# Zero products at five norms, a third weight unit of the second expert ahead, masks between the projection chunks

## What is computed

```python
def first_block(x, ...):
    for i in range(2):
        h = rmsnorm(x, norm_mix[i])
        y = gated_deltanet_bidir(h, ...) if i == 0 else dilated_window_attention(h, ...)
        x = x + y
        x = x + squared_relu_mlp(rmsnorm(x, norm_mlp[i]), w1[i], w2[i])   # 1024 -> 4096 -> 1024
    return rmsnorm(x, norm_final)

def gated_deltanet_bidir(h, w_in, conv_w, ...):
    qkv, z, ab = split(h @ w_in)                 # 3072, 1024, 32 columns
    qkv = silu(conv over 5 tokens (qkv))
    ...                                          # gated delta rule, both directions, chunked
def second_block(x, c, positions, ...):
    cos, sin = rope_tables(positions, 32)
    for l in range(2):
        sh1, sc1, g1, sh2, sc2, g2 = split(silu(c) @ w_mod[l] + b_mod[l])
        h = rmsnorm(x, norm1_g[l]) * (1 + sc1) + sh1
        x = x + g1 * ((three gated branches of h @ w_in[l]) @ w_out[l])
        h2 = rmsnorm(x, norm2_g[l]) * (1 + sc2) + sh2
        x = x + g2 * ec_moe(h2, ...)             # 16 experts, each takes its 32 best tokens
def ec_moe(h, w_router, w_gate, w_up, w_down):   # each weight 1024 x 1024 per expert
    ...
    y = (silu(xg @ w_gate[e]) * (xg @ w_up[e])) @ w_down[e]
```

## Time and profile before

| | us |
|---|---|
| median of 3 runs | 2377.35 |
| lowest and highest | 2376.77, 2383.16 |
| the profiled execution | 2378.3 |
| its span | 2376.3 |

### The profile page before, as it was taken

One profiled execution on the slowest core, in us unless ns is written; L12 is line 12 of the kernel. 1 busy time (PEld: TensorE's weight loads), 2 busy tenths in 40 slices (PEclk: granted clock), 3 DMA queues, 4 the chain that ended last, 5 costly groups with the idle time before them and its releaser, 6 DMA issues.

```text
span 2376.3 us, 34628 instructions
## 1 busy us (share of the span) xinstructions
PE 1977.1 (83%) x14616; PEld 1365.1 (57%) x14616; DVE 916.6 (39%) x1646; ACT 632.9 (27%) x1065; POOL 32.5 (1%) x51
## 2 busy tenths in 40 slices
PE   8898889999889998999886666667999886666665
PEld 7776758878557886898642222224888752222221
DVE  5655645668463766545410000002554520000001
ACT  3322344431134443374320000002374420000000
POOL 0100000000000000000000000000000000000000
PEclk9989999999999999999798888888999889888888
DMA  9301135769754775523599999999442669999997
GB/s 325 125 27 38 38 133 187 285 222 339 282 203 142 261 255 188 197 72 126 228 387 425 427 427 426 427 425 399 161 142 107 248 267 425 427 426 426 427 426 311
DMA packets 150883, 641.88 MB, mean 270 GB/s; under 512 B 9374, under 2 KB 30904, under 8 KB 117622
## 3 DMA queue, kind: packets, MB, share of 16 engines
q1 hardware_dynamic: 144474, 637.13, 67.9%
q10 hardware_dynamic: 6300, 3.20, 0.5%
HBM read 639.21 MB, written 1.10 MB: 269 GB/s over the span
## 4 chain that ended last, share of the span: by engine, by line
PE 57%; DMA 33%; DVE 5%; ACT 2%; issue 2%; DVEq 1%; SPq 1%; POOL 0%; ACTq 0%; POOLq 0%
DMA ring<-in_w_down 33%; PE psum L1377 6%; PE psum L992 5%; PE psum L993 5%; PE psum L994 5%; PE psum L1513 4%; PE psum L1095 3%; PE psum L691 3%; PE psum L1367 2%; PE psum L1256 2%; PE psum L1255 2%; PE psum L1257 2%; PE psum L1112 1%; PE psum L761 1%; PE psum L1246 1%
## 5 line engine op out<-in xcount | busy, mean ns | idle before, releaser
L1493 PE MATMUL psum<-ring,arena 128*32 128x256 f32 x4096 | 292.5, 438 | 169.3 <-DMA ring<-in_w_up 130.1
L1493 PEld LDWEIGHTS psum<-ring,arena 128*32 128x32 f32 x4096 | 142.1, 123 | 322.1 <-issue 144.7
L1513 PE MATMUL psum<-ring,arena 128*32 128x512 f32 x1024 | 161.8, 763 | 95.3 <-DMA ring<-in_w_down 86.0
L992 PE MATMUL psum<-arena_r 128*128 128x512 f32 x512 | 206.2, 403 | 11.8 <-DVE arena_r L1937 7.1
L2341 DVE TENSOR_TENSOR arena<-psum,arena 128x256 f32<-128x256 f32 x32 | 13.6, 425 | 524.5 <-PE psum L1493 524.5
L994 PE MATMUL psum<-ring_r,arena_r 128*128 128x512 f32 x512 | 203.5, 397 | 0.0
L1626 DVE TENSOR_TENSOR ring_r<-ring,arena_r 128x2048 fp32r<-128x2048 f32 x64 | 143.7, 2287 | 85.7 <-ACT arena_r L2413 85.6
L2348 DVE TENSOR_TENSOR arena<-psum,arena 128x512 f32<-128x512 f32 x64 | 44.3, 692 | 267.8 <-PE psum L1513 266.5
L1513 PEld LDWEIGHTS psum<-ring,arena 128*32 128x32 f32 x1024 | 32.3, 124 | 189.3 <-DMA ring<-in_w_down 101.9
L2847 ACT ACTIVATE arena<-psum 128x256 f32<-128x256 f32 x32 | 12.3, 385 | 476.1 <-PE psum L1493 476.1
L2413 ACT CAST arena_r<-ring 128x2048 fp32r<-128x2048 f32 x64 | 119.5, 1903 | 71.6 <-PE psum L994 71.6
(11 more groups left out here) (404 smaller groups left out, 3399.5 us busy)
## 6 DMA issues: line engine op xcount, KB each, us to landing
ring<-in_w_up SPq DMA_DIRECT2D x64, 2048.0 KB, 26.1
ring<-in_w_down SPq DMA_DIRECT2D x64, 2048.0 KB, 26.5
ring<-in_w_gate SPq DMA_DIRECT2D x60, 2048.0 KB, 26.6
ring<-in_mlp_w SPq DMA_DIRECT2D x32, 2048.0 KB, 8.5
ring<-in_w_mod SPq DMA_DIRECT2D x24, 2048.0 KB, 11.3
ring<-in_w_in SPq DMA_DIRECT2D x20, 2048.0 KB, 8.4
ring<-in_gdn_w_in SPq DMA_DIRECT2D x8, 2048.0 KB, 18.0
ring<-in_dswa_w_in SPq DMA_DIRECT2D x9, 1536.0 KB, 13.2
```

The costliest lines, as they stand in the source:

```text
L992: mm(o, xh, wh, start=start, stop=False, skip_group_check=True)
L1493: ins = mm(PS[32 * j:32 * j + 32, 4 + m, 0:T], XG[:, k, 0:CAP] if first else XGE[:, k, :], W(v + 2 * m + u, D)[:, kk, j * T:(j + 1) * T], ...
L1513: ins = mm(PS[32 * j:32 * j + 32, (7, 4)[half], :], HTE[:, k % 2, 32 * (k // 2):32 * (k // 2) + 32], W(v + 4 + u, D)[:, j, half * 512:(hal ...
```

## The change

Three things are done together.

**Zero products.** `keep_busy(n, b)` issues n products of 128x128 by 128x256 in f32, both operands the one column of zeros `zero1` repeated, into PSUM bank b, with no wait ahead. There are 2 before the transposes of MLP 0, 10 before those of MLP 1, 18 and 11 before those of the two layers of the second block, and 6 between the two halves of the attention norm. PE waits for POOL's first memsets once, at the start.

**Third unit.** A new buffer `NEXT2` takes the first half of w_up of expert 1. SP issues it before the first unit of expert 0, ACT copies it into its slot behind the two gate units, and SP's `expert(1, 3)` begins with the second up unit. To make room, the scratch space for GpSimd's own transfers, which the kernel has none of, is set to 256.

**Masks and loads.** `masks_and_angles` is cut in five and run behind the convolutions of chunks 10, 12, 14, 16 and 18. On SP the three `PMC` loads go behind the units `U_QKV + 1` and `U_QKV + 2`, which move ahead of them. PE waits for the ten small loads ahead of the decay sums.

```diff
@@ -191,6 +191,7 @@
 
         slots = [both(f"ring{i}", [P, SLOT]) for i in range(RING)]
         ring, ring_r = [s[0] for s in slots], [s[1] for s in slots]
+        NEXT2 = sb("next_up", [P, SLOT])[:]
         X = sb("x_resid", [P, TT, D])
         XN, XN_R = both("x_normed", [P, TT, D])
         HT, HT_R = both("h_featmajor", [P, KC, T])
@@ -451,10 +452,6 @@
             sp.dma_start(ALOG, A["gdn_a_log"].rearrange("a b c -> a (b c)").partition_broadcast(P)[:, 0]).then_inc(sem("params_in"), 16)
             load(U_AB, cols(A["gdn_w_in"][0], 4096, 4128))
             load(U_QKV, cols(A["gdn_w_in"][0], 0, 512))
-            for name, width in (("b_mod_2", 96), ("norm1_g_2", 16), ("norm2_g_2", 16)):
-                at = PM_AT[name]
-                sp.dma_start(PMC[:, at:at + width].rearrange("p (m k) -> p m k", k=KC),
-                             A[name].rearrange("l (m p k) -> p (l m) k", p=P, k=KC)).then_inc(sem("gdn_in"), 16)
             sp.dma_start(CUM, A["k_gdn"][:, 0:2 * P].rearrange("p (a b) -> p a b", b=P)).then_inc(sem("gdn_in"), 16)
             sp.dma_start(NEGM, A["k_gdn"][:, 2 * P:4 * P].rearrange("p (a b) -> p a b", b=P)).then_inc(sem("gdn_in"), 16)
             sp.dma_start(EYE32, A["k_gdn"][:, 4 * P:4 * P + Q32]).then_inc(sem("gdn_in"), 16)
@@ -462,7 +459,13 @@
             sp.dma_start(NW, A["gdn_norm_w"].partition_broadcast(P)[:, 0]).then_inc(sem("gdn_in"), 16)
             for t in range(TT):
                 sp.dma_start(POSI[:, t:t + 1], A["positions_2"][0, t * P:(t + 1) * P].rearrange("(p a) -> p a", a=1)).then_inc(sem("gdn_in"), 16)
-            for u in range(1, 8):
+            load(U_QKV + 1, cols(A["gdn_w_in"][0], 512, 1024))
+            load(U_QKV + 2, cols(A["gdn_w_in"][0], 1024, 1536))
+            for name, width in (("b_mod_2", 96), ("norm1_g_2", 16), ("norm2_g_2", 16)):
+                at = PM_AT[name]
+                sp.dma_start(PMC[:, at:at + width].rearrange("p (m k) -> p m k", k=KC),
+                             A[name].rearrange("l (m p k) -> p (l m) k", p=P, k=KC)).then_inc(sem("gdn_in"), 16)
+            for u in range(3, 8):
                 load(U_QKV + u, cols(A["gdn_w_in"][0], 512 * u, 512 * (u + 1)))
 
             def mod(g):
@@ -547,14 +550,15 @@
                     for u in range(2):
                         load(U_SEC + V_MOE + 4 + u, two(A["w_down_2"])[u * 512:(u + 1) * 512, :].rearrange("(j p r) n -> p j (r n)", p=P, r=2), tu + e)
 
+                second = pmajor(one(A["w_gate_2"])[1])
+                sp.dma_start(NEXT2.rearrange("p (k n) -> p k n", n=D), pmajor(one(A["w_up_2"])[1])[:, 0:4, :]).then_inc(sem("next0_in"), 16)
                 expert(0, 0)
-                second = pmajor(one(A["w_gate_2"])[1])
                 sp.dma_start(NEXT0.rearrange("p (k n) -> p k n", n=D), second[:, 0:4, :]).then_inc(sem("next0_in"), 16)
                 for part, ks in ((1, slice(6, 7)), (2, slice(7, 8))):
                     sp.dma_start(NEXT1[part].rearrange("p (k n) -> p k n", n=D), second[:, ks, :]).then_inc(sem("next1_in"), 16)
                 sp.wait_ge(sem("router_mm"), L + 1)
                 sp.dma_start(NEXT1[0].rearrange("p (k n) -> p k n", n=D), second[:, 4:6, :]).then_inc(sem("next1_in"), 16)
-                expert(1, 2)
+                expert(1, 3)
                 with sp.Fori(2, NE) as e:
                     expert(e, 0)
             sp.dma_start(LAST_ROW, A["final_g_2"].rearrange("(a d) -> a d", a=1).partition_broadcast(P)[:, 0]).then_inc(sem("fgr_in"), 16)
@@ -632,11 +636,18 @@
             def used(ins, n):
                 ins.then_inc(w_free[n % RING], 1)
 
-            def norm(k, pm=False):
-
+            def keep_busy(n, b):
+
+                for _ in range(n):
+                    mm(bank(b, T), zero1.to_broadcast([P, P]), zero1.to_broadcast([P, T]), start=True, stop=True, skip_group_check=True)
+
+            def norm(k, pm=False, before=0, between=0):
+
+                keep_busy(before, 4)
                 pe.wait_ge(sem("xn0"), k + 1)
                 for t in range(TT):
                     if t == 1:
+                        keep_busy(between, 0)
                         pe.wait_ge(sem("xn1"), k + 1)
                     for dc in HT_ORDER if t == 1 else range(KC):
                         o = pair(4 + dc // 2, P)[:, (dc % 2) * 2 + t]
@@ -672,6 +683,7 @@
 
 
             pe.wait_ge(sem("params_in"), PARAMS)
+            pe.wait_ge(sem("filled"), 1)
             for n, group in enumerate(ROWS):
                 cnt = sum(x for _, x in group)
                 ins = nc.tensor.transpose(PS[:, 3, n * P:n * P + cnt], ROWS_IN[0:cnt, n * P:(n + 1) * P], ident[0:cnt, 0:cnt])
@@ -721,6 +733,7 @@
 
             def decay_sums():
 
+                pe.wait_ge(sem("gdn_in"), 16 * 10)
                 pe.wait_ge(sem("gs_ready"), 1)
                 for d in range(2):
                     rhs = GS[:, :, d * 8:(d + 1) * 8]
@@ -1050,6 +1063,7 @@
                             ins = nc.tensor.transpose(pair(6 + cc // 2, P)[:, (cc % 2) * 2 + t], RL[u % 2][:, t, cc * P:(cc + 1) * P], ident)
                     ins.then_inc(sem("rl_turned"), 1)
 
+                keep_busy((2, 10)[l], 4)
                 norm_split(k_norm, 0)
                 up(0, 0, 0)
                 up(1, 0, 1)
@@ -1074,7 +1088,7 @@
                 return
 
 
-            norm(2)
+            norm(2, between=6)
 
             def relative():
 
@@ -1234,7 +1248,7 @@
             for L in range(NL):
                 tu = L * SEC_TURNS
                 u2 = U_SEC
-                norm(L * 2 + 4, True)
+                norm(L * 2 + 4, True, before=(18, 11)[L])
 
                 def tok(n, w, b):
 
@@ -1676,21 +1690,27 @@
                 dst = KN[:, ch - GH] if ch < 2 * GH else V[:, ch - 2 * GH]
                 v.tensor_copy(dst, pair(4 + ch % 2, P)[:, 0:2]).then_inc(sem("tok_done"), 1)
 
-            def masks_and_angles():
+            TWO_PI = 2.0 * math.pi
+            c1 = 6.28125
+            c2_ = 0.0019350051879882812
+            c3 = TWO_PI - c1 - c2_
+            BIG = 12582912.0
+
+            def masks():
 
                 dve.wait_ge(sem("gdn_in"), 16 * 10)
                 v.tensor_copy(marks[:], MSTAGE)
 
-                TWO_PI = 2.0 * math.pi
-                c1 = 6.28125
-                c2_ = 0.0019350051879882812
-                c3 = TWO_PI - c1 - c2_
-                BIG = 12582912.0
+            def angles():
+
                 v.tensor_copy(POSF, POSI[:])
                 settle()
                 for t in range(TT):
                     v.tensor_scalar(ANG[:, t, :], freq, POSF[:, t:t + 1], None, ALU.mult)
                 settle()
+
+            def turns():
+
                 v.tensor_scalar(KRD, ANG, 1.0 / TWO_PI, BIG, ALU.mult, ALU.add)
                 settle()
                 v.tensor_scalar(KRD, KRD, BIG, None, ALU.subtract)
@@ -1698,12 +1718,18 @@
                 for cst in (c1, c2_, c3):
                     v.scalar_tensor_tensor(ANG, KRD, -cst, ANG, ALU.mult, ALU.add)
                     settle()
+
+            def quarter_turn():
+
                 v.tensor_scalar(COS, ANG, math.pi / 2, None, ALU.add)
                 settle()
                 v.tensor_scalar(KRD, COS, math.pi, None, ALU.is_gt)
                 settle()
                 v.scalar_tensor_tensor(COS, KRD, -TWO_PI, COS, ALU.mult, ALU.add)
                 settle()
+
+            def limits():
+
                 lim = 3.1415925
                 v.tensor_scalar(COS, COS, lim, -lim, ALU.min, ALU.max)
                 v.tensor_scalar(ANG, ANG, lim, -lim, ALU.min, ALU.max).then_inc(sem("angle_in"), 1)
@@ -1746,7 +1772,6 @@
                 v.tensor_tensor(flat(KD_S), PS[:, 6, 32:64], flat(GC), ALU.subtract).then_inc(sem("decay_in"), 1)
 
             decay_logits()
-            masks_and_angles()
             for ch in range(24):
                 conv(ch)
                 if ch - 3 >= GH:
@@ -1755,6 +1780,16 @@
                     decay_steps()
                 elif ch == 7:
                     decay_totals()
+                elif ch == 10:
+                    masks()
+                elif ch == 12:
+                    angles()
+                elif ch == 14:
+                    turns()
+                elif ch == 16:
+                    quarter_turn()
+                elif ch == 18:
+                    limits()
                 elif ch == 21:
                     keys_scaled()
             for ch in (21, 22, 23):
@@ -2854,7 +2889,7 @@
                 gathered(0, 0, 2 * CAP, first_place)
                 expert(0, 0)
                 gate0, gate1 = u2 + V_MOE, u2 + V_MOE + 1
-                act.wait_ge(sem("next0_in"), L * 16 + 16)
+                act.wait_ge(sem("next0_in"), L * 32 + 32)
                 a.copy(ring[gate0 % RING][:, 0:SLOT], NEXT0).then_inc(w_full[gate0 % RING], 16)
                 act.wait_ge(sem("next1_in"), L * 48 + 48)
                 at = 0
@@ -2862,6 +2897,8 @@
                     ins = a.copy(ring[gate1 % RING][:, at:at + part.shape[1]], part)
```

(4 more changed lines are left out.)

## The result

The changed kernel takes 2361.02 us in the median of four executions (2357.07 to 2366.59) against 2377.06 of the kernel before: ratio 0.9936, 95% interval 0.9922 to 0.9951, that is 15.2 us (11.6 to 18.5) less. The forecast was 2361.9 us, 15.5 us less. In a second series on one chip it was 2360.66 against 2375.36 (0.9931, 0.9918 to 0.9944). All ratios are of undisturbed executions: one of the twelve of the kernel with the products alone took 2514.18 us at a mean clock of 0.80 and stands in none.

The account below looks back on a forecast made before the run. Bound: the w_down loads of the expert stages at 426 GB/s, and PE for nearly all the rest. 1.6 + 7.6 + 6.3 = 15.5 us off the median of 2377.35 gave 2361.9 us; range 2357 to 2369.5.

Parts of the forecast that it names:

- The bound and its two levers: Whole kernel: w_down loads a third of the chain, nearly all the rest PE; cut or advance bytes, or cut PE time.
- Part 1: Kernel start: masks and angles moved between the chunks, net gain 1.6 us, bounds 0 to 1.8.
- The 1.8 at the start: Kernel start: the first convolution begins earlier, so PE no longer waits before its first transposes; 1.8 us gained.
- The 0.2 us lost behind chunk 10: Behind chunk 10: the 1.26 us mask cast overruns DVE's 1.08 us idle time, giving 0.2 us back.
- Part 2: Five norms: zero products fill PE's gaps and keep the clock high; 7.6 us gained, bounds 0 and 9.
- B: Norm gaps: zero products don't count as work at all, 1.9 us gain, 2375.4 us; chance 0.05.
- D: Norm gaps: a zero product costs double from the start, 0.86 us, total 2387.8 us; chance 0.04.
- Rival A: Norms: the clock falls in the transposes despite the zero products; 7.9 us remain, 2369.5 us; chance 0.15, whole or in part.
- the row that I set against it: Behind the 8.32 us gap: the clock rose at about 918.35, so the 3.65 us of transposes worked towards it.
- Part 3: Expert stages: half of expert 1's w_up loaded early; net 3.1 us a layer, 6.3 in two layers.
- the 4.92 us of one unit: Expert stage: one 2 MB unit fewer in the unbroken row of transfers at 426 GB/s, 4.92 us less.
- E: More gain: all three changes at upper bounds, 2359.7, plus fastest-run spread or less low clock ahead of experts; 2357 to 2360; chance 0.08.

Follow-up runs that it names:

- masks kernel: Only the moved masks and angles, with the loads and wait belonging to them, added to the kernel before: 2375.36 us (0.9991).
- unit kernel: Only the third unit of expert 1 sent ahead, added to the kernel before: 2368.64 us (0.9961).

## Why the prediction was right, step by step

- **The bound and its two levers** (fewer bytes in the row, PE at full clock elsewhere): right. PE's other idle time was left, and nothing new became the bound.
- **Part 1**, 1.6 us. The 1.8 at the start was 1.9, and only in executions in which PE comes early. (The pair of transposes took 0.38 us in the changed kernel, not the 0.22 of the sum; it is the product behind it that starts 0.22 us after it, where it was 0.28.) The 0.2 us lost behind chunk 10 didn't occur (the lead is 1.91 before and behind), but some 0.2 us went behind chunk 14 (one step of 4.63 instead of 4.39 us), where I had counted on 1.47 us of cover. The missing condition is that PE is early enough to be caught: I took one execution's start as fixed. The three loads were issued at 15.7, 22.4 and 29.1 us and PE passed its new wait without idle time at 40.4.
- **Part 2**, 7.6 us, measured 6.7 (4.0 to 9.3) alone. The term that I took without a row, 0.43 us for a product of zeros, was 0.43 to 0.44; rivals B and D are out by it. By norm, read from the traces: second MLP 29.98 to 27.01 us between transposes and hidden transposes (27.02 forecast), first layer 1.0 (1.0), second layer 2.0 (1.9), attention 1.5 (1.7: the chunk takes 3.69 us behind the filled gap, not the 3.46 of a projection chunk), first MLP 0 against the one profile of before. That last term is the weak one: the masks kernel and the unit kernel, without products, lose 1.5 to 1.7 us there, so the two products at the first MLP are worth something in some executions. I had read one execution and taken 1.17 us of idle time for harmless.
- **Rival A**: it fell with the row that I set against it. The clock held through every norm's transposes, and in 6.06 us of transposes alone. The Trainium skill (TensorE: Matmul & The Clock Gate, Part 4: PE-mode transpose) says that transposes don't count as activity in the same way. For these f32 transposes the traces don't agree with the rule. What I had read for A was also too strong: the attention chunk at 5.18 us is 1.5 times its full-clock time, not twice, since the clock was low from 525.8 to 529.2 us only.
- **Part 3**, 6.3 us. The row starts 1.72 us later against PE (1.78), the copy came 0.24 us early (0.1). From expert 1's start to the stage's last down unit it is 426.2 us in the mean of the three kernels without the unit (six stages) and 423.4 in seven with it (fourteen): 2.8 us a layer, where I had 3.1 and bounds of 2.9 to 3.4. The mis-sized term is the 4.92 us of one unit: from the row's first issue the saving was 4.6 and 4.0 us. Why the row gives back 0.3 to 0.9 us the runs don't show. Alone, part 3 measured 9.3 us with an interval from 6.0 to 12.6; the stages up to their last down unit explain 5.6. Counted to the end of the combination the same stages take 433.5 and 430.1 us in the mean, 3.4 us a layer or 6.8 in all, but that takes in the shorter last down unit, of which no run says whose it is.
- **The surplus of 5.8 us** in the profiled execution was none of E's causes; it lies where the clock's level differs from execution to execution, at the start of the recurrence and behind the last landings, and it was gone in the second one (span 2361.2). That the forecast and the median differ by 1 us is in part luck: part 1's gain depends on the start, and the interval is 7 us wide.

## What to carry to other kernels

Where PE waits between stages, look at the clock behind the gap and not only at the gap: zero products that end just before the data are ready cost nothing, and here they had to fill nearly all of it; too many are paid in full, and half as many gave most of the gain back. A short gap that looks harmless in one trace may not be so in the next, as at the first MLP. A fetch into a spare buffer is worth what it takes out of a row of transfers, less how much later the row then starts, and only where the queue is empty when it is sent. Before a gain at a kernel's start is counted, see whether PE reaches that place at the same time in every execution.

## What the runs showed of the hardware that I had not expected

- PE busy for 10.00 of 10.00 us was no sign of a full clock: 0.50 throughout with products of 128x64, and a fall some 3 us into products of 128x16.
- The kernel's first 32 small products take 3.9 to 5.0 us or 7.01 us, as the clock first rises at 12 to 14 us or at 24 to 25 us, and PE comes to its first transposes at 29.1 to 30.8 (31.0 with the wait of the kernel before) or at 32.6 to 33.1 us. The views print a clock of 1.00 ahead of the first record; the pace of the products shows that it was the low level.
- The clock can fall while PE works: it did, 0.7 us after it took up work behind 2.33 us of idle time, having been 1.00 in the idle time itself.
